# The down weights of the experts are requested by ScalarE on its own DMA queue instead of by SyncE

## The reference, cut to what matters

```
D_MODEL, D_EXPERT, N_EXPERTS = 1024, 512, 32          # 512 prompt tokens and 8 sample tokens
def hier_moe(x, g_ffn, w_group, w_router, w_gate, w_up, w_down):
    h = rmsnorm(x, g_ffn).reshape(b * t, d)
    ...                                               # router: two experts and their shares for each token
    def add_expert(acc, params):
        wg, wu, wd, c = params
        act = jax.nn.silu(h @ wg) * (h @ wu)
        return acc + (act @ wd) * c[:, None], None
    out, _ = lax.scan(add_expert, jnp.zeros_like(h), (w_gate, w_up, w_down, combine))
```

## Time and profile before

| | |
|---|---|
| median of three runs | 1336.88 us (1334.86 to 1337.11) |
| profiled execution, its own time | 1333.26 us |
| its span | 1331.5 us |
| mean granted clock of TensorE | 0.941 |
| busy in the span | PE 84%, DVE 37%, ACT 16%, POOL 14% |
| DMA | 304.13 MB moved, mean 228 GB/s |
| the chain that ended last | DMA 27% (the up weights 24%), PE 10% |

### The profile page before, as it was taken

How to read it: one execution, slowest core, us unless ns; L and a number is a source line. 1 busy time by engine, 2 the same in 40 slices (tenths; PEclk the granted TensorE clock), 3 DMA queues, 4 the chain that set the end, 5 groups by cost and what they waited for, 6 DMA issues and landing times. The chain is left out here.

```text
span 1331.5 us, 16132 instructions
## 1 busy us (share of the span) xinstructions
PE 1118.3 (84%) x6077; PEld 587.5 (44%) x6077; DVE 492.7 (37%) x1181; ACT 217.5 (16%) x478; POOL 187.3 (14%) x180
## 2 busy tenths in 40 slices
PE   4989999887799999988999747999777777777784
PEld 3544434333355454522355545555444444444442
DVE  3427967993486766522231362111111111111110
ACT  2112221111233333321000100111111001111110
POOL 1012101210000000000200101323222222222211
PEclk9989999998899999899999656999999999999997
DMA  5142022205364433569500692999999999999991
GB/s 172 31 139 88 5 91 80 80 17 191 104 213 149 145 96 95 187 229 379 192 1 1 270 427 103 400 396 393 403 404 408 400 404 403 404 400 404 403 387 44
DMA packets 76084, 304.13 MB, mean 228 GB/s; under 512 B 21366, under 2 KB 21366, under 8 KB 63718
## 3 DMA queue, kind: packets, MB, share of 16 engines
q1 hardware_dynamic: 60582, 273.46, 53.4%
q0 software_dynamic: 9824, 16.98, 4.5%
q10 hardware_dynamic: 5600, 12.65, 2.5%
HBM read 290.02 MB, written 29.66 MB: 240 GB/s over the span
## 5 line engine op out<-in xcount | busy, mean ns | idle before, releaser
L364 PE MATMUL p_z<-m_w,m_xT 128*128 128x512 f32 (+2 forms) x528 | 214.9, 563 | 5.1 <-DMA m_w<-in_w_in 4.5
L1641 PE MATMUL e_G<-x_ew,e_xT 128*64 128x256 f32 x1024 | 132.8, 413 | 41.6 <-DMA x_ew<-in_w_gate 40.8
L1641 PE MATMUL e_U<-x_ew,e_xT 128*64 128x256 f32 x1024 | 124.0, 393 | 27.1 <-DMA x_ew<-in_w_up 26.9
L364 PEld LDWEIGHTS p_z<-m_w,m_xT 128*128 128x128 f32 (+1 forms) x528 | 95.4, 194 | 113.3 <-issue 107.6
L1653 PE MATMUL e_Y<-x_ew,e_aT 128*64 128x512 f32 x512 | 118.6, 605 | 23.1 <-DVE e_aT L1780 23.1
L767 PE MATMUL a_G<-m_w,m_xT 128*128 128x512 f32 x256 | 130.0, 630 | 2.5 <-ACT k_x L825 2.5
L1641 PEld LDWEIGHTS e_G<-x_ew,e_xT 128*64 128x64 f32 x1024 | 86.1, 144 | 99.3 <-issue 66.9
L1771 DVE TENSOR_TENSOR e_den<-e_sig,e_G 128x256 f32<-128x256 f32 x32 | 13.5, 421 | 289.1 <-ACT e_sig L1736 281.9
L1641 PEld LDWEIGHTS e_U<-x_ew,e_xT 128*64 128x64 f32 x1024 | 71.7, 136 | 77.5 <-DMA x_ew<-in_w_up 37.1
L1741 ACT ACTIVATE e_y<-e_Y,x_share 64x512 f32<-64x512 f32 x64 | 43.7, 683 | 313.8 <-PE e_Y L1653 313.4
L1653 PEld LDWEIGHTS e_Y<-x_ew,e_aT 128*64 128x64 f32 x512 | 37.9, 138 | 81.7 <-issue 53.0
(11 more groups left out here) (331 smaller groups left out, 1313.9 us busy)
## 6 DMA issues: line engine op xcount, KB each, us to landing
x_ew<-in_w_gate SPq DMA_DIRECT2D x32, 2048.0 KB, 44.3
x_ew<-in_w_up SPq DMA_DIRECT2D x32, 2048.0 KB
x_ew<-in_w_down SPq DMA_DIRECT2D x32, 2048.0 KB, 45.0
m_w<-in_w_in SPq DMA_DIRECT2D x11, 2048.0 KB, 7.8
k_x<-in_cache_diff_k SPq DMA_DIRECT2D x32, 256.0 KB, 3.0
k_x<-in_cache_dsa_k SPq DMA_DIRECT2D x32, 256.0 KB, 2.7
g_page<-in_cache_diff_v SPq DMA_DIRECT2D x32, 256.0 KB, 4.4
g_page<-in_cache_dsa_v SPq DMA_DIRECT2D x32, 256.0 KB, 6.9
```

The costliest lines, as they stand in the source:

```text
L364: last = nc.tensor.matmul(z[u % 3][0:p, 0:WIDTH[k]], s.xT[:, j, 128 * i:128 * i + p], s.w[:, c % 2, j, 0:WIDTH[k]], start=j == 0, stop=j = ...
L1641: last = nc.tensor.matmul(pair(bank[CAP * h:CAP * h + CAP, 0:HW]), xT[:, j, b, :], own(s.ew[n][:, r, b, :], h), start=b == 0, stop=b == KD ...
```

## The change

SP no longer requests the down weights of experts 3 to 31 in this stage. ACT does, on its own queue, in its list behind the two copies L1741 of expert e, for expert e + 3. It needs no wait of its own, since ACT has waited for `d_done` of expert e ahead of the copies. The requests of the first three experts, and those of the extra blocks, stay with SP.

```
@@ experts(), block.sync
             for e in range(DEPTH, NE):
-                for n, (wt, done) in enumerate(zip(EXPERT_WEIGHTS, (g_done, u_done, d_done))):
+                for n, (wt, done) in enumerate(zip(EXPERT_WEIGHTS[:2], (g_done, u_done))):
                     sp.wait_ge(done, e - DEPTH + 1)
                     sp.dma_start(s.ew[n][:, e % DEPTH], s.expert(io[wt], e, n)).then_inc(s.ew_in[n][e % DEPTH], 16)
@@ experts(), block.scalar
                 last.then_inc(y_out, 1)
+                if e + DEPTH < NE:
+                    act.dma_start(s.ew[2][:, e % DEPTH], s.expert(io["w_down"], e + DEPTH, 2)).then_inc(s.ew_in[2][e % DEPTH], 16)
```

## The result

The kernel before takes 1336.42 us in the median of four runs (1334.86 to 1337.11), the changed kernel 1349.75 us (1348.17 to 1353.08). The ratio is 1.0108, with a 95% interval of 1.0089 to 1.0126. By the medians that is +13.3 us; the prediction said +14.4. The profiled execution took 1349.15 us, and its span is 1347.3 us.

What follows compares the result with a forecast made beforehand. Weight reading was taken to bound the experts' stage at 16.57 us an expert; additions would then bind at 17.1 us, +14.4 us including the last transfer's +5.4. 1336.88 + 14.4 = 1351.3 us, range 1338 to 1367 us.

Steps and rivals of the forecast that it cites:

- The likeliest case: Experts' stage: additions bind at 17.1 us a step, over the weights' 16.57: +14.4 us; chance 45% for +6 to +28.
- The last transfer, +5.4 us: End of the weight stream: expert 31's up weights, not its down weights, land last, near 1310.1 us: +5.4 us.
- one of the last three would do so in either kernel, so I count no difference: Last three products: one following a PE wait takes longer, some 5.4 us where others take 3.8, in both kernels; counted 0.
- its two terms: End of the stage: the last transfer, +5.4 us; and the additions' step, +14.4 us with the first inside it.
- the first rival: Only the last transfer counts and the additions stay hidden: +5.4 us, 1342.3 us; chance 30% for +3 to +6.
- The additions, the other +9.0 us: POOL's additions: down-weight rows between their packets lengthen the step from 12.8 to 17.1 us, beyond the last transfer's share.
- the 0.8 an engine that the forecast took: Down-weight rows an engine moves before POOL's packets begin: less than one of eight, in the 1 us ahead.
- By the forecast's own count: Additions' step: each down-weight row between their packets costs a turn, 0.60 us; 7.2 rows add 4.3 us to 12.8.
- ACT's requests at nothing: ACT's 29 added requests, 0.34 us each, fit its 2.25 us idle before the next sigmoid: 0; without that cover 10 us.
- The rate: DMA rate with ACT's queue beside SP's: neither gain nor loss, from 428 GB/s with both queues against 431 with SP's alone.
- The rival "faster": Weight stream: two queues fill the engines better; 1.7% more rate would make the kernel 0.2% faster; chance 8%.

Runs made afterwards that it cites:

- The kernel with the last transfer alone: Kernel before, all weights on SP, but expert 31's down weights requested ahead of its gate and up weights: 1338.72 us against 1334.50, ratio 1.0032.
- the pair with three buffers: Changed kernel with three e_y buffers instead of two: 1341.65 us; the same with expert 31's down weights requested by SP, last: 1337.68 us.
- the early request: Changed kernel with ACT's request for down weights moved ahead of its wait for y_added: 1341.26 us against 1334.50, ratio 1.0049.
- the third buffer: Changed kernel with three e_y buffers, so ACT's copy waits for the additions of expert e - 3, not e - 2: 1341.65 us against 1335.46, ratio 1.0047.
- the pair without y_s: Kernel before and changed kernel, both without the experts' 32 additions to y_s: 1329.89 us and 1336.29 us, against 1335.46.
- the fourth place: Kernel before with a fourth down-weight place in k_x, expert 3's requested at stage start: 1336.08 us; requested behind the first turned rows: 1332.34 us.

## Why the prediction was right, step by step

**The likeliest case came, in sign, size and mechanism.** The additions bind: a step of 17.06 us where 17.1 were forecast, all requests held by the y_s addition, y_s landing after 14.2 us (14 to 15 forecast), ACT in its wait for an addition, PE's gate products without a wait for weights, q10 in turn with the two others. The last down product ends at 1331.3 (1329.9 forecast, and 2.1 us of the profile are from ahead of the stage). That the sum is so near, +14.4 against +13.3, is partly luck, as the terms below show: each is off by more than a microsecond.

**The last transfer, +5.4 us.** The mechanism was right and the size was off. The kernel with the last transfer alone is 4.2 us slower by its medians (3.4 us by its trace), and the pair with three buffers differs by 3.9 us. The step that was off is "one of the last three would do so in either kernel, so I count no difference": in the two traces, which of the three products is the long one makes 1.7 us, and 5.4 less 1.7 is 3.7.

**What the prediction left out between its two terms.** Where all down weights are ACT's and the additions don't bind, the loss is 6.3 to 6.5 us (the early request, the third buffer, the pair without y_s), with intervals of 2 to 3 us to either side, so that 5.4 is not excluded. The way is another, though: the traces of these kernels end with PE at its own pace behind late up weights of expert 29 or 30, not with a wait for the last transfer, since early down weights make the up weights of about every second expert late. A state in which the additions don't bind thus exists one small edit away, as the first rival had it, and costs about what the rival said.

**The additions, the other +9.0 us.** Measured some 7 us, roughly: 13.3 less 6.4. The forecast made the step from one landing to one request; the early request and the third buffer show that this tie is needed for it, since without it the mean step is under 16.5 us. The step of the argument that a landing releases ACT's copies, and these the request, carried it. But the hit of 17.06 on 17.1 is partly luck. The request goes out with the first copy and not 1.1 us later, as ACT's timeline shows:

```profile
923.66 0.68 ACT L1741 ACTIVATE e_y<-e_Y,x_share 64x512 f32<-64x512 f32 x1 [15.98 <-DMA out_y_s<-e_y,x_to_s]
923.71 0.33 ACTq L1745 DMA_DIRECT2D x_ew<-in_w_down  x1
```

So more rows pass ahead than the 0.8 an engine that the forecast took: from 1044 to 1046.5 us, before POOL's first packet, there are 27 packets of q10 on the 16 engines, 1.7 each (25 to 27 at two other experts). By the forecast's own count 6.3 rows are then left, 3.8 us, and the step would be 16.6 us, at which the additions cost nothing. Single steps go down to 16.0 us, but the mean is 17.06, and what makes up the other 0.5 us isn't shown.

**ACT's requests at nothing.** Right: 0.33 to 0.35 us each, beside the copy; the first sigmoid starts 2.25 us after the copies as in the earlier trace rows. It holds for one request an expert. With four an expert the sigmoid waited up to 16.3 us.

**The rate.** Right within what it claims: 397 against 402 GB/s, a DMA share of 1.00 against 1.01. The rival "faster" has nothing for it. The turns count one packet of each queue, 79, 76 and 72, as the profile counts packets. The figure of 9 to 17 descriptors in a packet in the Trainium skill's "DMA: Bandwidth & Descriptors" (Queues, rings and completion order) doesn't fit this either if a descriptor is a row: an engine passed only some 5 rows of each queue in the 6 us. How many descriptors make a row no view here shows. Its rule that spreading transfers over SP, ACT and GpSimd doesn't help the bandwidth (Rules for kernel authors) agrees with the 397 GB/s; it says nothing of what the third queue loses.

**Not foreseen.** PE waits 25 times for gathered rows, 78.2 us in all, as the gather stands behind the additions in POOL's queue. Until expert 28 it lies inside the step that the additions set; at the end one such wait, of 3.06 us, stands on the chain. It costs 0.4 us there, since the hidden rows of that expert are ready only at 1299.50, and are turned from 1299.90 on.

**Open.** Why the last down product of the kernel before starts 1.8 us earlier without y_s; what the 0.5 us in the step of the additions are; what the lower granted clock costs where the additions don't bind; what sets the number of requests at which ACT's queue holds its engine.

## What to carry to other kernels

A transfer moved to another queue was paid for here by the queue with the many small packets. So count that queue's packets, multiply by the largest packet of each queue with which it will now share the turns, and compare the longer step with the pace that hides it (12.8 us lay under the weights' 16.6, 17.1 above it). Look whether the request and the small transfers are released by the same event, since then they meet every time; a request moved by one wait, or one more buffer, won half of the loss back. The order in one queue is also a schedule: what is last in it should be what is needed last. A stream that was a whole transfer shorter, with the fourth place, gained nothing, because the last weights in it were needed 5.4 us earlier than the ones before.

## What the runs showed of the hardware beyond what was expected

- A DMA request behind a computation in ACT's list goes out with the start of it: 834.69 us beside a copy that starts at 834.68, and within 0.05 us of it at 28 of the 29 experts (0.33 at the other). It has no wait of its own for the copy.
- A request can hold its engine. With four requests of 4 KB rows an expert, two of them took 12.30 us on ACT, the longer of the two 6.26; with two of 8 KB rows the pair took at most 1.86 us, and single ones of 16 KB rows take 0.34.
- Three queues take turns one packet at a time, whatever the size, by the profile's count: 79 and 76 packets of mostly 16 KB and 72 of 1.5 KB on the mean in the same 6 us.
- A first gather of POOL is delayed as well by a weight transfer requested at the same time: PE waits 10.03 us for it in the kernel with the fourth place and 6.55 before, 3.5 us more.
- The granted clock of TensorE falls when PE works again after a long wait: 0.93 in the 6.0 us of a wait for up weights, 0.50 (1.2 GHz) in the 2.5 us behind it, and the up product takes 6.64 us instead of 3.79.
